# The sums of the modulation over the partitions: made by GpSimd's all-reduce in place of TensorE's transposes and products with ones

## The reference, cut to what matters

```
c_act = silu(c)                                   # 1 x 2048
mod = (c_act @ w_ada + b_ada)                     # 2048 x 12288 weights, 96 MB
sh1, sc1, gt1, sh2, sc2, gt2 = split(mod, 6)      # 2048 numbers each
h = rms_norm(x, g_pre_mix) * (1 + sc1) + sh1      # needed at the start of the second block
...                                               # projections, two attentions, gates, w_o -> mix
x = x + gt1 * rms_norm(mix, g_post_mix)
h = rms_norm(x, g_pre_ffn) * (1 + sc2) + sh2      # needed before the feed-forward part
...                                               # w_up, convolution, silu, w_down -> y
x = x + gt2 * rms_norm(y, g_post_ffn)
```

## Time and profile before

| what | value |
|---|---|
| median of 3 runs | 1902.23 us (1901.94 to 1903.13) |
| the profiled execution's own time | 1901.29 us |
| its span, first to last instruction | 1899.6 us |
| granted TensorE clock | 1.00 of full speed, mean over the span |
| DMA, mean over the span | 233 GB/s |

### The profile page before, as it was taken

How to read it: one execution, slowest core, us unless ns; L and a number is a source line. 1 busy time by engine, 2 the same in 40 slices (tenths; PEclk the granted TensorE clock), 3 DMA queues, 4 the chain that set the end, 5 groups by cost and what they waited for, 6 DMA issues and landing times.

```text
span 1899.6 us, 29882 instructions
## 1 busy us (share of the span) xinstructions
PE 1885.5 (99%) x9895; PEld 1600.7 (84%) x9895; DVE 1365.6 (72%) x1889; ACT 1038.8 (55%) x1689; POOL 102.5 (5%) x168
## 2 busy tenths in 40 slices
PE   9999999999999999999999999999999999999998
PEld 7888888888889988888888788888888888888886
DVE  7777777887767556678777877777777766655555
ACT  6545546654545544457654445666566666544444
POOL 3000001000000112211100000000000000000000
PEclk9999999999999999999999999999999999999999
DMA  8888787798777754476678885777777766465553
GB/s 304 288 307 263 247 268 264 267 350 278 265 266 231 233 169 130 136 224 203 216 251 287 302 296 176 233 244 232 232 236 240 232 199 188 160 205 191 195 195 137
DMA packets 233225, 443.52 MB, mean 233 GB/s; under 512 B 14363, under 2 KB 108197, under 8 KB 232000
## 3 DMA queue, kind: packets, MB, share of 16 engines
q1 hardware_dynamic: 229840, 428.27, 68.2%
q0 software_dynamic: 3248, 14.29, 2.4%
q10 hardware_dynamic: 64, 0.02, 0.0%
HBM read 438.28 MB, written 4.24 MB: 233 GB/s over the span
## 4 chain that ended last, share of the span: by engine, by line
PE 97%; DVE 1%; ACT 1%; issue 0%; DMA 0%; ACTq 0%; DVEq 0%
PE PS L2071 57%; PE PS L2561 17%; PE PS L2565 9%; PE PS L2441 3%; PE PS L2451 2%; PE PS L2230 1%; PE PS L2239 1%; PE PS L2126 1%; PE PS L2249 1%; PE PS L2250 1%; PE PS L2247 1%; PE PS L2217 1%; PE PS L2219 1%; PE PS L2135 0%; PE PS L2206 0%
## 5 line engine op out<-in xcount | busy, mean ns | idle before, releaser
L2071 PE MATMUL PS<-w_hi,aT 128*128 128x512 f32 (+1 forms) x3264 | 1045.0, 394 | 1.7 <-DVE w_lo L1280 0.8
L1280 DVE TENSOR_TENSOR w_lo<-raw,w_hi 128x1024 fp32r<-128x1024 f32 (+2 forms) x624 | 754.5, 1213 | 387.2 <-ACT w_hi L730 379.6
L730 ACT ACTIVATE w_hi<-raw 128x1024 fp32r<-128x1024 f32 (+2 forms) x624 | 651.1, 1047 | 568.2 <-PE PS L2071 319.2
L2071 PEld LDWEIGHTS PS<-w_hi,aT 128*128 128x128 f32 x3264 | 611.7, 188 | 132.1 <-issue 5.4
L2071 PE MATMUL PS<-w_lo,aT 128*128 128x512 f32 (+1 forms) x1632 | 633.0, 388 | 0.0
L2561 PE MATMUL PS<-aT,w_hi 128*128 128x512 f32 x1408 | 442.9, 396 | 1.1 <-DVE aT L1449 1.1
L2071 PEld LDWEIGHTS PS<-w_lo,aT 128*128 128x128 f32 x1632 | 307.0, 188 | 58.9 <-issue 0.2
L2565 PEld LDWEIGHTS PS<-aT,w_lo 128*128 128x128 f32 x1408 | 264.5, 188 | 62.5
L2565 PE MATMUL PS<-aT,w_lo 128*128 128x256 f32 x1408 | 276.6, 278 | 0.0
L1338 DVE SCALAR_TENSOR_TENSOR arena<-ada_raw,silu_c,arena 128x1024 f32<-128x1024 f32 x192 | 246.3, 1283 | 28.7 <-DMA ada_raw<-in_w_ada 28.0
L2561 PEld LDWEIGHTS PS<-aT,w_hi 128*128 128x128 f32 x1408 | 214.4, 189 | 1.8 <-issue 1.8
(11 more groups left out here) (271 smaller groups left out, 1389.9 us busy)
## 6 DMA issues: line engine op xcount, KB each, us to landing
raw<-in_w_in SPq DMA_DIRECT2D x248, 512.0 KB, 4.4
ada_raw<-in_w_ada SPq DMA_DIRECT2D x192, 512.0 KB, 4.9
raw<-in_w_up SPq DMA_DIRECT2D x176, 512.0 KB, 3.6
raw<-in_w_down SPq DMA_DIRECT2D x88, 512.0 KB, 4.0
raw<-in_w_out SPq DMA_DIRECT2D x32, 512.0 KB, 5.7
raw<-in_w_o SPq DMA_DIRECT2D x32, 512.0 KB, 6.1
raw<-in_w_uq SPq DMA_DIRECT2D x24, 384.0 KB, 3.7
raw<-in_w_ukv SPq DMA_DIRECT2D x16, 512.0 KB, 5.2
```

The costliest lines, as they stand in the source:

```text
L730: nc.scalar.activation(part_of(w_hi, m, width), part_of(raw, m, width), ACT.Copy).then_inc(hi_ready, 1)
L1280: nc.vector.tensor_tensor(part_of(w_lo, m, width), part_of(raw, m, width), part_of(w_hi, m, width).bitcast(F32), ALU.subtract).then_inc(lo ...
L2071: mm = pe.matmul(dst, l, r, start=first and j == 0, stop=last and j == 2)
```

## The change

The accumulators stay, and DVE's multiplying and adding into them. Every sum over the partitions is made by one POOL instruction, `partition_all_reduce`, 128 x 2048 from SBUF to SBUF, which leaves the sum in all partitions. There are seven: sh1, sc1, sc2, the two halves of sh2, gt1, gt2. For the five that are needed as columns, POOL then makes everything zero but each partition's own column of every tile (`own_columns`, an affine_select on the spot), and DVE adds up along the free axis from SBUF. The gates are used as they come. Of the sixteen loads for sh2's second half, which stood in the first three w_o panels, eight are moved ahead into the last four gates panels, two each (slots 1 and 5), and the rest stand in the first two w_o panels; the seam gets 24 transposes in place of the product with ones.

```diff
+            def whole(dst, acc):
+                nc.gpsimd.partition_all_reduce(dst, acc, P, bass.bass_isa.ReduceOp.add).then_inc(pool_step, 1)
+                pool.wait_ge(pool_step, T.ready(pool_step))
+            def own_columns(t):
+                t = t.rearrange("p (k n) -> p k n", k=KT)
+                nc.gpsimd.affine_select(out=t, in_=t, compare_op=ALU.is_equal, fill=0.0, base=0,
+                                        pattern=[[0, KT], [1, P]], channel_multiplier=-1).then_inc(ada_whole, 1)
+                pool.wait_ge(ada_whole, T.ready(ada_whole))
...
             T.skip(pool_step, 15)
-            pool.wait_ge(mod_ready, 2)
+            gate_pieces = credits["ada_done"] + 64 + OUT_PIECES
+            pool.wait_ge(ada_done, gate_pieces - 4)
+            pool.wait_ge(rows_T, T_SEAM_2)
+            whole(SUM_SH1, ADA_1[:, 0:D])
+            own_columns(SUM_SH1)
+            pool.wait_ge(ada_done, gate_pieces - 1)
+            whole(SUM_SC1, ADA_1[:, D:2 * D])
+            own_columns(SUM_SC1)
             nc.gpsimd.memset(ADA_SH2[0], 0.0).then_inc(acc_zeroed, 1)
...
                 nc.gpsimd.dma_start(x1_dram[s * P:(s + 1) * P, :], X[:, s, :]).then_inc(x_saved, 16)
+            pool.wait_ge(ada_done, credits["ada_done"] + 64 + 32)
+            whole(SUM_SC2, ADA_SC2)
+            own_columns(SUM_SC2)
...
+            pool.wait_ge(ada_done, credits["ada_done"] + 64 + 32 + 16)
+            whole(SUM_SH2[0], ADA_SH2[0])
+            own_columns(SUM_SH2[0])
             pool.wait_ge(q_out, 12)
...
+            pool.wait_ge(ada_done, credits["ada_done"] + 64 + 32 + 16 + 32 + 8)
+            nc.gpsimd.partition_all_reduce(SUM_GT1, ADA_GT1, P, bass.bass_isa.ReduceOp.add).then_inc(gt1_summed, 1)
+            pool.wait_ge(gt1_summed, 1)
             pool.wait_ge(rows_T, T_SEAM_4)
...
+            pool.wait_ge(ada_done, credits["ada_done"] + 64 + 96)
+            whole(SUM_SH2[1], ADA_SH2[1])
+            own_columns(SUM_SH2[1])
...
+            pool.wait_ge(ada_done, credits["ada_done"] + 64 + 96 + 32)
+            nc.gpsimd.partition_all_reduce(SUM_GT2, ADA_GT2, P, bass.bass_isa.ReduceOp.add).then_inc(gt2_summed, 1)
...
-            def mod_sums(part, bank):
-                dve.wait_ge(ada_cols, T.ready(ada_cols))
+            def mod_sums(part, src, before=None):
+                dve.wait_ge(ada_whole, T.ready(ada_whole))
                 total = tmp_b[:, 0, :]
-                link(nc.vector.tensor_reduce(total, PS[:, bank:bank + 4, :].rearrange("p b (k n) -> p (b k) n", k=4),
-                                             AX.X, ALU.add))
+                nc.vector.tensor_reduce(total, src.rearrange("p (k n) -> p k n", k=KT), AX.X, ALU.add)\
+                    .then_inc(ada_cols_read, 1)
...
-        O_PIECES = ((0, 2, 4, 6), (0, 1, 2, 4, 5, 6), (0, 1, 2, 4, 5, 6), ())
+        O_PIECES = ((0, 2, 4, 6), (0, 2, 4, 6), (), ())
...
+                    if slot in (1, 5):
+                        ada(ADA_SH2[1], slot // 5, p + SLOTS)
...
             def o_slot(slot):
                 sh2_piece(0, slot)
-                if slot in (3, 6):
...
+                if slot == 6:
+                    dve.wait_ge(row_landed, 16)
+                    dve.wait_ge(gt1_summed, 1)
+                    link(nc.vector.tensor_tensor(G_MIX, SUM_GT1, G_MIX, ALU.mult))
...
+                    if p == 2 and slot == 3:
+                        mod_sums(SH2, SUM_SH2[1], mod[:, SH2, :])
...
-            dve.wait_ge(g_copied, 1)
-            link(nc.vector.tensor_tensor(G_FFN, ADA_GT2, G_FFN, ALU.mult))
+            dve.wait_ge(ffn_gain_landed, 16)
+            dve.wait_ge(gt2_summed, 1)
+            link(nc.vector.tensor_tensor(G_FFN, SUM_GT2, G_FFN, ALU.mult))
...
-            ada_transpose(ADA_1[:, 0:D], B_ROT)
...
-                    spread(ADA_GT1, B_SPREAD, (0, 1) if slot == 2 else (2, 3))
...
-            ada_reduce(ADA_SH2[1])
-
+            keep_busy(24, 2)
...
-                    spread(ADA_GT2, 0, range(4))
+            pe.wait_ge(conv_sum, credits["conv_sum"] + FT - 2)
```

More of the change, by code:

```diff
@@ L173, in block_kernel @@
         ADA_GT2 = arena[:, 17408:17408 + D]
+        SUM_SH1, SUM_SC1, SUM_SC2 = [arena[:, at:at + D] for at in (8192, 10240, 12288)]
+        SUM_SH2 = [arena[:, at:at + D] for at in (16384, 14336)]
+        SUM_GT1 = arena[:, 4096:4096 + D]
+        SUM_GT2 = ada_raw[:, :, :].rearrange("p a n -> p (a n)")
         stage = sb("stage", [P, ST, 2, HD])
@@ L341, in block_kernel @@
         THIRD_PIECES = (0, 4)
-        O_PIECES = ((0, 2, 4, 6), (0, 1, 2, 4, 5, 6), (0, 1, 2, 4, 5, 6), ())
+        O_PIECES = ((0, 2, 4, 6), (0, 2, 4, 6), (), ())
         def late_piece(p, slot):
-            n = sum(len(q) for q in O_PIECES[:p]) + O_PIECES[p].index(slot)
+            n = 8 + sum(len(q) for q in O_PIECES[:p]) + O_PIECES[p].index(slot)
             return SLOTS + n // 2, n % 2
@@ L498, in _, with gt1_and_sh2 @@
             panels(4, W_IN2, C_G, upto(W_IN2, C_G + D), ada_piece(GT1, 0), free_ada_done=4)
-            panels(4, W_IN2, C_G + D, upto(W_O, 0), ada_piece(GT1, 16), free_ada_done=4)
+            gt1 = ada_piece(GT1, 16)
+            def gt1_and_sh2(i, slot):
+                gt1(i, slot)
+                if slot in (1, 5):
+                    load_ada(i * P + SLOTS * P, SH2 * D + 1024 * (slot // 5))
+            panels(4, W_IN2, C_G + D, upto(W_O, 0), gt1_and_sh2, free_ada_done=6)
             def load_up(j, c0):
@@ L1102, in _ @@
             act.wait_ge(lat_inv, 1)
+            act.wait_ge(ada_cols_read, 3)
             for g in range(4):
@@ L1217, in up_panel @@
                             y_split(slot - 4, slot - 2)
[L1218 to L1221, removed]
                     if last and slot == 7:
@@ L1678, in _ @@
             turned_panel(lambda slot: ada_piece(ADA_SC2, 0, slot, OUT_PIECES), lambda: add_out(0, 2))
-            mod_sums(SH1, B_ROT)
+            mod_sums(SH1, SUM_SH1)
             for slot in range(SLOTS):
@@ L1684, in _ @@
                 ada_piece(ADA_SC2, 0, slot, OUT_PIECES + 4)
-            mod_sums(SC1, B_ROT)
+            mod_sums(SC1, SUM_SC1)
             for slot in range(SLOTS):
@@ L1744, in _ @@
                 if j == 7:
-                    mod_sums(SC2, B_UP1)
+                    mod_sums(SC2, SUM_SC2)
                     gain(1, C_PREFFN, SC2)
@@ L1783, in qs_out @@
                 copy_out(lambda s: QS[:, s, ds(p * PANEL, PANEL)])
-            panel(0, ("mla", 0), None, qs_out)
+            panel(0, ("mla", 0), None, lambda p: (mod_sums(SH2, SUM_SH2[0]), qs_out(p)))
             with T.loop(3, **DP, **HEADS4, ready_dve_step=8) as i:
@@ L2172, in turned_panel @@
                         transpose_group(slot + 4, src, banks=B_ROT)
[L2174 to L2193, removed]
             def head_T(kind, j=0):
@@ L2341, in values, with panel @@
                 return lambda s: KVS[:, s, ds(i * SWA_D + SWA_G * SWA_D, SWA_D)]
-            def panel(start=None, before=None, columns_read=None):
+            def panel(start=None, before=None):
                 for slot in range(SLOTS):
                     chunk(slot, KT)
-                    if columns_read is not None and slot == 0:
-                        pe.wait_ge(mod_ready, columns_read)
                     if h := due(slot, 4, start, before):
@@ L2376, in _ @@
                 T.skip(acc_free[s], 1, "free")
-            pe.wait_ge(ada_done, credits["ada_done"] + 64 + OUT_PIECES)
-            ada_transpose(ADA_1[:, 0:D], B_ROT)
-            for slot in range(SLOTS):
-                chunk(slot, KT)
-            pe.wait_ge(mod_ready, 1)
-            ada_transpose(ADA_1[:, D:2 * D], B_ROT)
-            for slot in range(SLOTS):
-                chunk(slot, KT)
+            for _ in range(2):
+                for slot in range(SLOTS):
+                    chunk(slot, KT)
             for slot in range(SKEW):
@@ L2486, in _ @@
                     first, last = kt == 0, kt == VT - 1
-                    if first and g == 2:
-                        pe.wait_ge(mod_ready, 4)
-                        pe.wait_ge(ada_done, credits["ada_done"] + 64 + 32 + 16)
-                        ada_transpose(ADA_SH2[0], B_UP1)
                     pe.wait_ge(lo_ready, T.ready(lo_ready))
@@ L2508, in _ @@
             pe.wait_ge(v_out, 8)
-            panel(("mla", 0), columns_read=6)
+            panel(("mla", 0))
             for i in range(3):
```

64 lines of the change are left out of this document (17 added, 47 removed).

## The result

The changed kernel takes 1947.11 us (median of 4 runs, 1945.81 to 1947.74), the one before 1902.33: a ratio of 1.0235, 95% interval 1.0222 to 1.0248. I had said 1919, 17.9 us slower by my sum; it is 44.5 slower (profiled executions; 44.8 by the medians). The direction was right, which I had given a chance of 0.51; the size was not: more than twice the forecast. The time lies in the range of 1887 to 1980, but that range held "faster" and "slower" alike. The profiled execution took 1945.81 us, its span is 1944.1. One of the twelve executions of experiment 9 took 6671.82 us and counts neither in its range nor in its ratio.

The account below looks back on a forecast made before the run. PE, busy 99% of the span, was taken to bound the kernel. 1901.3 - 13.1 us of removed PE work + 31.0 of stalls from held DVE splits = 1919.2, said as 1919; range 1887 to 1980.

Parts of the forecast that it names:

- 7T - 34: PE's added waits beside the seven sums, T being one all-reduce's length on POOL: 31.0 us in all.
- PE's work, -13.1: Transposes removed from PE for the sums save 13.1 us; the seam was taken to give nothing.
- An all-reduce holds DVE's splits: DVE's splits, with two operands in SBUF, stand still for the whole length of each all-reduce on POOL.
- my first rival: DVE isn't held, or not for long, so only the 13.1 us saved on PE count: 1888; chance 0.40.
- T = 9.3: Length in us of one 128 x 2048 all-reduce on POOL, taken as two passes at the two-operand pace.
- about one and a half microseconds of work in hand: At sc1, right behind sh1, PE's lead is used up but this work remains, so sc1 costs 7.8 us.
- the ring's lead of 5.6: In gates panels DVE's split chunks are ready 5.6 us before PE needs them, from a ring of four places.
- The clock "at nothing": Stalls might lower PE's clock from 2.4 to 1.2 GHz; taken as no cost, upper end 31 us.
- The family that I held likeliest: DVE held beside each sum, T from 7.3 to 18: 1905 to 1980 us; chance 0.38.
- rival 2: All-reduce much longer, seven halvings one after another, 35 us: 2099; chance 0.13 with what lies between.
- rival 3: DVE isn't held but the sums come late, with T of 22: 1899; chance 0.09 together with T of 6.2 to 7.3.

Follow-up runs that it names:

- experiment 9: Changed kernel with identity by DMA, all-reduces in eighths, sh2's second sum read later; DVE also meets sh1 and sc1 a panel later, gt1 in quarters: 1900.43 us.
- experiment 1: Changed kernel with each all-reduce replaced by seven memsets of its destination, selects and waits kept: 1891.71 us, ratio 0.9949.
- experiment 3: Changed kernel with each all-reduce cut into four of 512 columns, back to back on POOL: 1923.59 us, ratio 1.0117.
- experiment 4: Changed kernel with two more all-reduces of 1024 columns behind gt1's, which nothing waits for: 1955.40 us.
- experiment 6: Changed kernel with each all-reduce cut into eight of 256 columns: 1920.88 us.
- experiment 7: Changed kernel with all-reduces in eighths, the identity loaded by DMA, and sh2's second sum read three slots later: 1911.12 us, ratio 1.0048.
- experiment 8: Changed kernel without POOL's five selects, so the modulation is wrong, all-reduces whole: 1945.40 us.

## Why the prediction was right or wrong

Three steps failed: the lower clock, taken at nothing; the start, not in the sum at all; and the term of the stalls, 7T - 34, which came out too small.

- **PE's work, -13.1: right.** It is -14.0. The 0.9 more is the seam: 3.5 us of products gave way to 2.5 of transposes, which I had priced at nothing because the idle takes the rest. PE's wait there did grow as forecast, from 1.1 to 2.0.
- **An all-reduce holds DVE's splits: right** (experiments 1, 3, 4). The Trainium skill's lock ("SBUF — State Buffer", section "SBUF: two separate sides") was the better guide than my first rival: the trace agrees that DVE is kept out, now beside an instruction of 11.9 us. It speaks of the full instruction, though, and here DVE came free 9.0 us after the start of gt1's, gt2's and sc2's alike; the traces show the end of the waiting split, not the lock. PE's releaser was `w_lo`, as I had said, in four of the seven stalls; in sh1's and gt1's it was `aT`, in sc1's an emptied accumulator (L1709).
- **T = 9.3: too short for the instruction, near for the hold, by luck.** The instruction lasts 11.9, the hold 9.0. The two passes that gave 9.3 say nothing of DVE's coming free before the end.
- **7T - 34 = 31.0: mis-sized; 37.0 measured.** With the hold of 9.0 it says 29. Two terms failed. sc1: "about one and a half microseconds of work in hand" was 0.4, since PE ran dry at 444.6 and the all-reduce began at 444.23. PE then waited not for the held instruction, a product of DVE, but for the emptying of its accumulator behind it, done 1.9 us after DVE was free again; 11.4 in place of 7.8. gt1: I took the ring's lead of 5.6, but PE stood for `aT` (L1450), the transposed rows that DVE splits in the same queue and that have no ring; 6.3 in place of 3.6. sh1 and sc2 (3.1 for 4.0 each) and gt2 (2.8 for 3.6) came out lower, sh2's halves higher (5.0, 5.4 for 4.0).
- **The clock "at nothing": failed, 12.6 us.** I had it in the text with an upper end of 31 and chose zero, because no idle before the change was longer than 2.0 us (2.3 in truth). Nothing in those rows bore on an idle of 3 to 11 us; the stalls that I forecast were outside what they cover. The middle would have been a better choice than the end.
- **The start: missing, 8.7 us.** I asked what each new operation costs where it stands, and not what it costs that the program holds it. And I misread the waits: PE's longest of all isn't the 2.0 us for a DMA but the 2.3 us for POOL's identity. It is the wait that became 13.0; 2.0 of the 10.7 more fell on the wait for the DMA, which is gone. That row said that PE's start hangs on POOL and has no slack. The length of the delay no row before the change could tell.

So the miss of 26.6 us (17.9 by the sum, 44.5 measured) is 12.6 of clock, 8.7 of start, 6.0 of stalls and 0.2 of other waits, less the 0.9 that PE's work fell more. The family that I held likeliest, DVE held and PE waiting beside each sum, is the one that came. Of the rivals, 1 (DVE not held) is refuted by the split of 9.41 us and by experiments 3 and 4, 2 by the 11.9 us, 3 as the cause by experiment 1 (and in the changed kernel DVE waits for POOL nowhere); its mechanism appears once the sums are cut and so last 15 to 17 us (6, 7), and goes when they are met later (9).

## What to carry to other kernels

Before moving work to an idle engine, ask which of the busy engines it shuts out and for how long at a stretch: one instruction of 12 us costs more than eight of 2 us, because a lead of 5 us covers a gap and not a stall. Then follow the stall: PE's idle was paid a second time at the lower clock, 12.6 us for 37.0 here, some 5 us more in experiment 8. And price an operation that is new to the program at its start too, where everything waits, and look there first for whom PE waits.

## What the runs showed of the hardware

- An all-reduce of 128 x 2048 floats takes 11.9 us, of 512 columns 3.22 from start to start, of 256 columns 1.77 at the least (experiment 6, 546.92 to 548.69 us): by an estimate from these three, 0.3 us of each are fixed.
- A memset of 128 x 2048 (1.8 us) leaves DVE's splits at 1.22 us (experiment 1); a select of the same tile in place holds a split of DVE for 1.8 of its 2.4 us.
- An instruction of DVE with an operand in PSUM isn't held: 0.68 us beside the all-reduce of sh2's second half (1137.11 us), 0.67 and 0.68 beside the pieces of experiment 9 (431.73 and 432.32 us).
- A program with one all-reduce anywhere has its first select on POOL 10.1 to 12.2 us late; memsets ahead of it are not late. In the changed kernel POOL also stands idle for 8.0 to 11.4 us later on, ahead of two of its adds and of one all-reduce.
